# Two decoder layers on one core: other places for layer 0's value and gate splits, and norm sums as rows turned to columns

## The reference

```
for l in range(2):
    ada = silu(c) @ W_ada[l] + b_ada[l]     # shift, scale, gate for two sub-layers
    u = x*(1+sc1)+sh1;  x = LayerNorm(alpha*x + (1+g1)*Mixer(u))
    u = x*(1+sc2)+sh2;  x = LayerNorm(alpha*x + (1+g2)*SwiGLU(u))
```

## Time and profile before

| | us |
|---|---|
| runs (3) | 1695.4 median, 1695.18 to 1696.8 |
| profiled execution, its own time | 1694.97 |
| its span | 1693.2 |
| PE busy | 1629.9 (96%) |
| PEld busy | 1290.8 (76%) |
| DVE busy | 1001.0 (59%) |
| ACT busy | 623.4 (37%) |
| chain that ended last | PE 89%, DVE 5%, ACT 2%, DMA 1% |

### The profile page before, as it was taken

How to read it: one execution, slowest core, us unless ns; L and a number is a source line. 1 busy time by engine, 2 the same in 40 slices (tenths; PEclk the granted TensorE clock), 3 DMA queues, 4 the chain that set the end, 5 groups by cost and what they waited for, 6 DMA issues and landing times.

```text
span 1693.2 us, 21286 instructions
## 1 busy us (share of the span) xinstructions
PE 1629.9 (96%) x8391; PEld 1290.8 (76%) x8391; DVE 1001.0 (59%) x1548; ACT 623.4 (37%) x1117; POOL 51.6 (3%) x102
## 2 busy tenths in 40 slices
PE   6899999999999999999989999999999999999997
PEld 3678766677778888888878777766778788888886
DVE  3677677758676565555557657766557533333344
ACT  3332454444253332222253325445533533222221
POOL 1000000000000000000000000000000000000000
PEclk8999999999999999999999999999999999999999
DMA  9664221134327666665416331111223233334232
GB/s 306 186 183 138 75 63 52 50 100 132 107 60 211 186 188 187 186 184 149 148 51 191 87 88 38 39 38 31 82 87 100 62 100 99 100 96 122 88 94 73
DMA packets 278450, 193.07 MB, mean 114 GB/s; under 512 B 8344, under 2 KB 264912, under 8 KB 278352
## 3 DMA queue, kind: packets, MB, share of 16 engines
q1 hardware_dynamic: 264112, 147.95, 30.1%
q0 software_dynamic: 12320, 43.11, 8.6%
q10 hardware_dynamic: 1920, 0.66, 0.2%
HBM read 189.59 MB, written 2.10 MB: 113 GB/s over the span
## 4 chain that ended last, share of the span: by engine, by line
PE 89%; DVE 5%; ACT 2%; DMA 1%; issue 1%; SPq 0%; DVEq 0%; ACTq 0%
PE banks L1553 23%; PE banks L1555 22%; PE banks L1554 22%; PE banks L1671 3%; PE banks L1702 3%; PE banks L1730 2%; DMA ada_first<-in_w_ada_dram 1%; PE banks L1587 1%; PE banks L1588 1%; PE banks L1591 1%; PE banks L1606 1%; PE banks L1608 1%; PE banks L1607 1%; PE banks L1677 1%; PE banks L1681 1%
## 5 line engine op out<-in xcount | busy, mean ns | idle before, releaser
L1553 PE MATMUL banks<-u_hi,w_hi 128*128 128x512 f32 x1144 | 470.6, 411 | 14.9 <-DVE w_lo L941 11.6
L941 DVE TENSOR_TENSOR w_lo<-ring,w_hi 128x1024 fp32r<-128x1024 f32 (+2 forms) x246 | 294.4, 1199 | 309.6 <-ACT w_hi L687 308.3
L1555 PE MATMUL banks<-u_hi,w_lo 128*128 128x512 f32 x1144 | 449.2, 393 | 0.0
L1554 PE MATMUL banks<-u_lo,w_hi 128*128 128x512 f32 x1144 | 449.1, 393 | 0.0
L687 ACT ACTIVATE w_hi<-ring 128x1024 fp32r<-128x1024 f32 (+2 forms) x246 | 253.9, 1033 | 210.3 <-PE banks L1555 77.2
L1553 PEld LDWEIGHTS banks<-u_hi,w_hi 128*128 128x128 f32 x1144 | 216.5, 189 | 66.4 <-DVE w_lo L941 11.6
L1555 PEld LDWEIGHTS banks<-u_hi,w_lo 128*128 128x128 f32 x1144 | 216.3, 189 | 46.8
L1554 PEld LDWEIGHTS banks<-u_lo,w_hi 128*128 128x128 f32 x1144 | 217.3, 190 | 35.5
L833 ACT ACTIVATE probs<-banks,neg_max 128x128 f32<-128x128 f32 (+3 forms) x192 | 99.0, 524 | 159.6 <-DVE neg_max L1342 159.6
L1553 PE MATMUL banks<-h_hi,w_hi 128*128 128x512 f32 x352 | 138.5, 394 | 0.0
L1555 PE MATMUL banks<-h_hi,w_lo 128*128 128x512 f32 x352 | 137.0, 389 | 0.0
(11 more groups left out here) (240 smaller groups left out, 2159.3 us busy)
## 6 DMA issues: line engine op xcount, KB each, us to landing
ring<-in_w_ffn_in_dram SPq DMA_DIRECT2D x88, 512.0 KB, 3.9
ada_ring<-in_w_ada_dram POOLq DMA_DIRECT2D x80, 512.0 KB, 4.3
ring<-in_w_in_dram SPq DMA_DIRECT2D x72, 512.0 KB, 3.8
ring<-in_w_ffn_out_dram SPq DMA_DIRECT2D x32, 448.0 KB, 3.4
ada_first<-in_w_ada_dram SPq DMA_DIRECT2D x16, 512.0 KB, 8.3
ring<-in_w_out_dram SPq DMA_DIRECT2D x16, 512.0 KB, 3.6
ring<-in_w_ffn_out_dram SPq DMA_DIRECT2D x16, 512.0 KB, 4.1
w<-in_cmp_w_k_dram SPq DMA_DIRECT2D x8, 512.0 KB, 5.2
```

The costliest lines, as they stand in the source:

```text
L941: V.tensor_tensor(lo, src, hi.bitcast(fp32), ALU.subtract).then_inc(split_lo, 1)
L1553: M(bank, wh[:, block], sh[:, k, :], start=start, stop=False)
L1554: M(bank, wh[:, block], sl[:, k, :], start=False, stop=False)
L1555: return M(bank, wl[:, block], sh[:, k, :], start=False, stop=stop)
```

## The change

Four edits. (1) In layer 0 the splits of `vsg0`, `vsg1`, `vsg2` and `qn0` are placed by hand: VectorE does `vsg0` ahead of the set-up, `vsg1` between the two `build_flat`, `vsg2` behind them, `qn0` between the ropes of `ksl` and `kwn`; ScalarE does `vsg0` behind the copy of `kc`, `vsg1` ahead of `kwn`'s copy, `vsg2` and `qn0` behind it. The clearing of `v_cmp` moves up. (2) In the inner norms the sums are made by `rows`: 32 columns of `ones` stationary, 128 data columns moving, four groups of tokens into four groups of 32 partitions; VectorE copies the 128x128 result to `ln_rows`, TensorE transposes it, VectorE reads one column of each group. The order of the sums, the places of `keep_busy` (2, 2 and 7 instead of 8) and its bank change. (3) ScalarE's high half of the third job moves behind all squares; VectorE's low half is made in two halves, ahead of `u_lo` of block 0 and of block 1; `project_first` waits for each half where it reads it. (4) The sum of the last conditioning group moves from `kwn` to `qd3` of layer 1, its save from behind `qn1`'s rope to `vd1`.

```diff
-                "kwn": 9}
+ADA_SUM_WITH = {..., (0, "fo3"): 8, (1, "qd3"): 9}
...
+FIRST_LAYER_SPLIT = [(0, name) for name in ("kwn", "vsg0", "vsg1", "vsg2", "qn0")]
...
@@ scalar: layernorm
-                    if m == KD - 1 and not last:
-                        prepare(l + which, FIRST_SPLIT[which])
...
+                if not last:
+                    prepare(l + which, FIRST_SPLIT[which])
                 act.wait_ge(var_ready, n + 1)
@@ scalar: start of a layer
                 nc.scalar.activation(cmp_raw[:, 0, :], bank_of(l, "kc"), ACT.Copy)...
+                if l == 0:
+                    prepare(0, "vsg0")
...
                 for r, name in enumerate(RAW[:2]):
+                    if l == 0 and name == "kwn":
+                        prepare(0, "vsg1")
                     save_raw(l, name, r)
+                if l == 0:
+                    prepare(0, "vsg2")
+                    prepare(0, "qn0")
@@ vector: layernorm
-                if not last_norm:
-                    prepare(l + which, FIRST_SPLIT[which])
...
                 dve.wait_ge(mean_done, n + 1)
+                V.tensor_copy(ln_rows[:, 0, :], mean_rows).then_inc(mean_rows_saved, 1)
+                dve.wait_ge(var_done, n + 1)
+                V.tensor_copy(ln_rows[:, 1, :], square_rows).then_inc(square_rows_saved, 1)
+                dve.wait_ge(mean_col_turned, n + 1)
                 V.tensor_copy(mean_s, mean_col).then_inc(mean_saved, 1)
                 dve.wait_ge(mean_saved, n + 1)
                 link(V.tensor_tensor(square_s, mean_s, mean_s, ALU.mult))
-                dve.wait_ge(var_done, n + 1)
-                V.tensor_tensor(var_s, var_col, square_s, ALU.subtract).then_inc(var_ready, 1)
+                dve.wait_ge(square_col_turned, n + 1)
+                V.tensor_tensor(var_s, square_col, square_s, ALU.subtract).then_inc(var_ready, 1)
...
+                    if m in (1, 2):
+                        prepare_half(l + which, FIRST_SPLIT[which], m - 1)
                     if m:
                         sub_layer_low(n + 1, m - 1)
+            def prepare_half(l, name, half):
+                n, part = split_job(l, name), slice(half * SLOT // 2, (half + 1) * SLOT // 2)
+                ...
+                dve.wait_ge(split_hi, n + 1)
+                V.tensor_tensor(lo[:, part], src[:, part], hi[:, part].bitcast(fp32), ALU.subtract)\
+                    .then_inc((third_half, split_lo)[half], 1)
@@ vector: start of layer 0
             prepare(0, "kwn")
+            V.memset(v_cmp[:, :, :], 0.0)
+            prepare(0, "vsg0")
             V.memset(d_mix[:, 0:1], 0.0).then_inc(part1, 1)
...
                 build_flat(1)
+                if l == 0:
+                    prepare(0, "vsg1")
                 dve.wait_ge(kc2_ready, l + 1)
                 build_flat(0)
+                if l == 0:
+                    prepare(0, "vsg2")
...
                 for r, name in enumerate(("ksl", "kwn")):
                     prepare_behind(l, name)
+                    if l == 0 and name == "kwn":
+                        prepare(0, "qn0")
...
-                    elif i == 1:
-                        save_ada(9)
...
-                    if l == 0 and name == VD[1]:
-                        save_ada(0)
+                    if name == VD[1]:
+                        save_ada(9 * l)
@@ tensor: project_first
+                    for name, bank in zip(names, out):
+                        if name in THIRD and k == 0:
+                            pe.wait_ge(third_half, 2 * l + THIRD.index(name))
+                        elif k == (KD // 2 if name in THIRD else 0):
+                            take_split(l, name)
@@ tensor: mean_and_variance
+                def rows(out, src, start, stop):
+                    for i in range(TT):
+                        ins = M(out[32 * i:32 * i + 32, :], ones[:, 0:32], src[:, i * P:(i + 1) * P],
+                                start=start, stop=stop)
+                    return ins
...
                 pe.wait_ge(y_summed, n + 1)
-                columns(mean_col, t2, True, False)
+                rows(mean_rows, t2, True, False)
+                wait_saved(pe, l, ("wo", "fo")[which] + str(KD - 2))
+                keep_busy(2)
+                wait_saved(pe, l, ("wo", "fo")[which] + str(KD - 1))
+                rows(mean_rows, res[:, KD - 1, :], False, True).then_inc(mean_done, 1)
                 pe.wait_ge(sq_summed, n + 1)
-                columns(var_col, squares[:, 0, :], True, False)
-                wait_saved(pe, l, ("wo", "fo")[which] + str(KD - 1))
-                columns(mean_col, res[:, KD - 1, :], False, True).then_inc(mean_done, 1)
+                rows(square_rows, squares[:, 0, :], True, False)
                 pe.wait_ge(squared, (n + 1) * KD)
-                columns(var_col, squares[:, KD - 1, :], False, True).then_inc(var_done, 1)
+                rows(square_rows, squares[:, KD - 1, :], False, True).then_inc(var_done, 1)
+                pe.wait_ge(mean_rows_saved, n + 1)
+                nc.tensor.transpose(mean_turned, ln_rows[:, 0, :], ident).then_inc(mean_col_turned, 1)
+                pe.wait_ge(square_rows_saved, n + 1)
+                nc.tensor.transpose(square_turned, ln_rows[:, 1, :], ident).then_inc(square_col_turned, 1)
                 pe.wait_ge(mean_saved, n + 1)
                 spread(mean_ps, 0).then_inc(mean_spread, 1)
+                keep_busy(2)
                 pe.wait_ge(rstd_saved, n + 1)
                 spread(rstd_ps, 3).then_inc(rstd_spread, 1)
-                keep_busy(8)
+                keep_busy(7)
```

More of the change, by code:

```diff
@@ L136, in prepared_at @@
             nl, ni = divmod(l * len(SPLIT) + i + NQ - 1, len(SPLIT))
-            if nl < DEPTH and SPLIT[ni] not in FIRST_SPLIT and (nl, SPLIT[ni]) != (0, "kwn"):
+            if nl < DEPTH and SPLIT[ni] not in FIRST_SPLIT and (nl, SPLIT[ni]) not in FIRST_LAYER_SPLIT:
                 out.append((nl, SPLIT[ni]))
@@ L182 @@
 ADA_FFN = 3
-ADA_SUM_WITH = {"qd3": 0, "gm14": 1, "wo2": 2, "fb6": 3, "fb10": 4, "fb14": 5, "fb18": 6, "fb21": 7, "fo3": 8,
-                "kwn": 9}
-ADA_SUM_LAYER = {g: int(name == "kwn") for name, g in ADA_SUM_WITH.items()}
+ADA_SUM_WITH = {(0, "qd3"): 0, (0, "gm14"): 1, (0, "wo2"): 2, (0, "fb6"): 3, (0, "fb10"): 4, (0, "fb14"): 5,
+                (0, "fb18"): 6, (0, "fb21"): 7, (0, "fo3"): 8, (1, "qd3"): 9}
 FIRST = ("kc", "vc", "ksl")
@@ L257, in build @@
         w1_all = at("w1", 20, 16)
+        ln_rows = at("ln_rows", 16, 1)[:, 0, 0:2 * P].rearrange("p (k n) -> p k n", n=P)
         hid_rep_all = at("hid_rep", 8, 1)
@@ L358, in build @@
         rows_ps, cols_ps = banks[:, 6, :], banks[:, 7, :]
-        shift_ps, mean_col, var_col = banks[:, 2, :], banks[:, 3, 0:TT], banks[:, 4, 0:TT]
+        shift_ps = banks[:, 2, :]
+        mean_rows, square_rows = banks[:, 3, 0:P], banks[:, 4, 0:P]
+        mean_turned, square_turned = banks[:, 3, P:2 * P], banks[:, 4, P:2 * P]
+        mean_col, square_col = (b.rearrange("p (i n) -> p i n", i=TT)[:, :, 0] for b in (mean_turned, square_turned))
         third_ps, rstd_ps, mean_ps = banks[:, 5, :], banks[:, 6, :], banks[:, 7, :]
@@ L393, in build @@
         split_lo = sem("split_lo")
+        third_half = sem("third_half")
         part_read = sem("part_read")
@@ L436, in build @@
         sq_summed = sem("sq_summed")
+        mean_rows_saved = sem("mean_rows_saved")
+        square_rows_saved = sem("square_rows_saved")
+        mean_col_turned = sem("mean_col_turned")
+        square_col_turned = sem("square_col_turned")
         mean_saved = sem("mean_saved")
@@ L620, in load_slices @@
             def load_slices(first, last):
-                for n in range(first * KD, last * KD):
+                for n in range(first, last):
                     (l, j), k = ADA_GROUPS[n // KD], n % KD
@@ L1165, in _ @@
                                 1.0 - LAMBDA_INIT[l], None, ALU.mult)
-            V.memset(v_cmp[:, :, :], 0.0)
             dve.wait_ge(const_in, 32)
@@ L1519, in sum_ada @@
             def sum_ada(l, name, m):
-                g = ADA_SUM_WITH.get(name)
-                if g is None or ADA_SUM_LAYER[g] != l:
+                g = ADA_SUM_WITH.get((l, name))
+                if g is None:
                     return
@@ L1578, in project_first @@
             def project_first(l, names, src, high, ready, count):
-                w = [take_split(l, name) for name in names]
                 out = [take_bank(l, name) for name in names]
@@ L1585, in project_first @@
                     pe.wait_ge(high, count + k + 1)
-                    for bank, (wh, wl) in zip(out, w):
+                    for name, bank in zip(names, out):
[3 more added lines that the diff above has]
+                            take_split(l, name)
+                        wh, wl = split_slot(l, name)
                         M(bank, wh[:, block], sh[:, k, :], start=k == 0, stop=False)
@@ L1589, in project_first @@
                     pe.wait_ge(ready, count + k + 1)
```

(7 more changed lines are left out.)

4 lines of the change are left out of this document (3 added, 1 removed).

## The result

The changed kernel takes 1685.8 us (median of 4 runs, 1684.9 to 1686.8), the kernel before 1696.1 beside it (4 runs, 1695.2 to 1697.8): ratio 0.9935, 95% interval 0.9923 to 0.9947. The forecast was 1685.2. The profiled execution took 1685.16 with a span of 1683.3, against 1694.97 and 1693.2: 9.9 us of span to explain, 10.2 had been forecast.

A forecast was written before the change was run, and what follows sets the result against it. TensorE, busy 96% of the span, was taken as the bound, so only its gaps and clock matter. Gains 6.8 + 3.1 + 0.3 = 10.2 off 1694.97 give 1684.8, median 1685.2 us; range 1682.0 to 1689.3.

The forecast's parts named there:

- Part 1: Layer 0's value splits: earlier low halves on VectorE close TensorE's wait at the value products; gain 6.8 us.
- The rival of a late landing: Layer 0: `vsg2` or `qn0` lands 6 us or more behind issue, TensorE waits at `qn0`; 1688.7 us, chance 0.09.
- Part 2: Inner norms' sums as `rows`, 0.42 us each: first real product's L1102 1.4 us earlier at full clock, 0.6 at low.
- the 1.2 us that I had set beside the sum: Inner norms: two tiling switches on the path per norm, 0.19 each, 1.2 us less gain over three norms; left out.
- Parts 2 and 3: Inner norms: sums as `rows` plus third block's low half in two loop pieces; together 3.1 us over three norms.
- the middle: Gain per inner norm taken as 1.05 us, between 1.5 at full clock and 0.6 to 0.7 at low.
- Part 4: Last conditioning group's eight transposes leave layer 1's `kwn`, at low clock, for a full-clock place: gain 0.3 us.
- if the gap behind the norm then starts warm: Addition to the clock-up rival: clock high at the gap behind the norm, somewhat faster still, 1682 instead of 1683.0 us.
- 5.54 + 24 x 0.096: Layer 0's values: upper bound of the gain if every wait went, given as 7.9 us.
- the clock stays up in all norms: Rival: full clock in all norms and no wait left at `qn0`; 7.9 + 4.2 + 0.3, 1683.0 us, chance 0.10.
- The halves eat the norms' gain: Rival: slower copies and turns, or low clock in all three norms, leave the norm edits about zero; 1688.3 us, chance 0.18.
- The slower one: Rival: four groups of `rows` run in line at low clock, 5.0 us a norm lost; 1703.3 us, chance 0.03.

The follow-up runs named there:

- splits alone: The kernel before with only layer 0's new split places and the moved clearing of `v_cmp`: 1688.2 us, ratio 0.9951.
- columns kept: The changed kernel with all four norm sums by `columns`, no copies, turning or idle pairs, eight idle products behind the spreads: 1691.2 us, ratio 0.9966.
- whole third block ahead: The changed kernel with the third job's high half back ahead of ScalarE's square and both low-half pieces ahead of the statistics: 1685.4 us, ratio 0.9933.
- last group at its old place: The changed kernel with the last conditioning group's transposes back at `kwn` of layer 1: 1682.3 us, ratio 0.9919.
- in the gap: The changed kernel with the last conditioning group's eight transposes in layer 1's idle gap behind `project_first`: 1684.0 us, ratio 0.9924.
- `kwn` first: The changed kernel with ScalarE making `kwn`'s high half ahead of the copies of `kc` in layer 1: 1682.1 us, ratio 0.9909.

## Why the prediction was right, and where it was not

**Part 1 was right in size and place.** Forecast 6.8, measured 6.65 to 6.7 in two kernels. The steps, with this execution 1.6 us later at the start: values forecast from 61 to 73.5, seen from 62.62 to 75.08; 0.13 apart; waits at `qn0` and `qn1` forecast at 0.5 and 0.7, seen 0.46 and 0.44. The low halves were ready at 58.27, 66.43, 69.07, 75.65 and about 81.85 (`vsg0` to `qn1`), which is 1.67, 1.63, 1.37, 1.75 and 1.75 behind the forecast: all of it the late start, to 0.3. VectorE's queue, summed job by job from its own rows, gives this stretch. The rival of a late landing fell: ScalarE waited for two landings (4.01 and 2.46 us) but had `vsg2`'s high half done at 68.1 and `qn0`'s at 71.6, with VectorE there at 68.3 and 74.4, for `vsg2` with only 0.2 us to spare.

**Part 2, the size of a `rows` was right:** 0.42 forecast, 0.42 and 0.43 seen. The Trainium skill, page TensorEngine Tiling (Array Packing), section Key Properties, has a change of tiling mode drain TensorE. Here the first `rows` starts 0.32 us behind the product before it (475.29 to 475.61), where two products are 0.23 apart, so at this switch the trace shows 0.1 us at the most, and the 1.2 us that I had set beside the sum for that rule did not come.

**Parts 2 and 3 were right in the steps, and took the wrong share of the clock.** The reciprocal was forecast at 3.3 and the first L1102 at 4.1 to 4.9 behind the last add (3.27 and 4.26 seen), the end of `project_first` at +23.1 (504.0), seen +23.26. But the gain I took was the middle of 1.5 (full clock) and 0.6 to 0.7 (low), 1.05 a norm; measured were 1.32, 1.28 and 0.95 (3.55 against 3.1). The step that failed is the middle: the clock stays up in every norm with rows and the seven idle products (three norms in each of ten profiled executions) and fell in every norm with columns (three in each of three: before, splits alone, columns kept).

And most of the gain is this clock, which I had held for a modifier of it. I compared an end at the high level with one that had run at the low and put the difference down to the shorter chain. The whole third block ahead shows it: its reciprocal is at +4.06, as in the splits alone (+4.07), so nothing is earlier when the spreading starts; yet its first norm ends at +23.43 and theirs at +24.74. The splits alone, then the whole third block ahead:
```profile
480.55 3.65 PE L1795 MATMUL banks<-merged_hi 128*128 128x512 f32 x8
481.72 0.82 ACT L696 ACTIVATE u_hi<-res,add_u,mul_u 128x512 fp32r<-128x512 f32 x1 [1.86 <-DVE res L1110]
...
484.04 0.40 PE L1602 MATMUL banks<-u_hi,w_hi 128*128 128x512 f32 x1
```
```profile
480.73 1.87 PE L1828 MATMUL banks<-merged_hi 128*128 128x512 f32 x7
481.80 0.81 ACT L704 ACTIVATE u_hi<-res,add_u,mul_u 128x512 fp32r<-128x512 f32 x1 [1.75 <-DVE res L1123]
482.87 0.47 PE L1626 MATMUL banks<-u_hi,w_hi 128*128 128x512 f32 x1 [0.28 <-ACT u_hi L704]
```
At the low level the eight idle products took 3.65 us and kept TensorE from the first real product until 484.04, 1.50 us after its `u_hi` was ready (482.54). At the high level the seven were through in 1.87, at 482.60, just as `u_hi` was ready (482.61); an eighth, at 0.23, would by this estimate still have ended ahead of the first product. That product comes at +8.21 and at +6.85, which is the 1.31 but for 0.05. So what the low clock cost in the old norm it cost through the idle products, which stood in the way; in the kernel before likewise (`u_hi` ready at +7.05, first product at +8.10). Whether the old sums with fewer idle products, or with none, would have given a part of this gain was not run and stays open.

The chain that is 0.8 us shorter adds 0.17. In the changed kernel `project_first` is held by VectorE's `u_lo` of block 1 (TensorE idles 0.19 for it at +10.05), which starts at +9.31, and at +9.33 with the third block ahead, where TensorE comes to it at +10.35 without a wait: work that is taken from ahead of the statistics and put into the loop delays `u_lo` by what it saved.

What keeps the clock up, rows or idle products, is half answered. With the four `rows` and no idle products the clock fell in one of three norms; with columns and eight idle products behind the spreads it fell in three of three. So the rows (with their copies and turning) matter most, the seven idle products perhaps something, on the one norm that fell, the two pairs nothing. Why one norm fell and two did not, at the same instructions, is open.

**Part 4 had the wrong sign**, and this is the step of the prediction that failed in its mechanism: "the clock was still low ..., for a place at the full clock: 0.3 us". I compared two prices of the transposes and did not ask what covered them. At `qd3` nothing does. The changed kernel there:
```profile
973.59 0.39 PE L1589 MATMUL banks<-u_hi,w_lo 128*128 128x512 f32 x1
973.82 0.27 PE L1565 MATMUL banks<-cst,ada_acc 128*128 128x128 f32 x1
973.85 0.47 PE L1587 MATMUL banks<-u_hi,w_hi 128*128 128x512 f32 x1
974.16 0.39 PE L1588 MATMUL banks<-u_lo,w_hi 128*128 128x512 f32 x1
...
974.62 0.27 PE L1565 MATMUL banks<-cst,ada_acc 128*128 128x128 f32 x1
```
From one transpose to the next are 0.80 us, where three products alone take 0.68: 0.125 each, 1.0 for the eight. At `kwn` they stood in front of value products that wait for VectorE anyway, so they cost nothing. Two experiments bear it out (147.01 at the old place, 147.08 in the gap, 148.12 at `qd3`).

**The sum came out so close by luck.** Forecast 10.2: 6.8, 3.1, 0.3. Measured: 6.7, 3.55, -1.1, then 1.7 behind the third norm, where the clock stays up behind the gap of 2.57 (my rival "if the gap behind the norm then starts warm" had 1.0 for it), 0.7 in small differences that I traced to no edit (0.2 ahead of the first norm, 0.5 in layer 1), less 1.65 at the start. The 1.65 is no work of the change: the changed kernel itself starts at 55.62 in one execution and at 54.05 in the other. The 1.7 cannot be called its work either: behind the third norm the clock stayed up with the columns kept, and fell with the last group at its old place and with `kwn` first, whose norms are the changed kernel's. Without the 1.65 the span would have been 11.5 shorter. Two small sums of the prediction are off and move nothing: 5.54 + 24 x 0.096 is 7.84 and not 7.9, and three norms at 1.5 are 4.5 where the rival has 4.2.

Of the rivals, "the clock stays up in all norms" held for the norms; its other half did not (the wait at `qn0` was 0.46), and it had 4.2 us for the three norms, which gave 3.55, and no loss in Part 4. "The halves eat the norms' gain" was true of the shortened chain (0.17 of the 0.8 left) and false of the time. The slower one asked for 2.3 us a norm; none was near.

## What to carry to other kernels

Before a few instructions are moved off a queue that waits, ask what covers them at the old place and at the new one: eight transposes of 0.125 us were free ahead of a wait, cost 1.1 us in a full stretch and were free again in a gap. Where a gap of the bounding engine is closed or shortened, count the clock behind it as well, and ask whether another engine then lets it be used: in layer 1 the full clock was worth nothing while VectorE's low half of `vsg2` set the pace, and with the splits placed earlier the stretch behind the gap gave more (3.7 us) than the gap itself (3.1). Idle products that are to hold the clock stand in the way when it falls all the same: eight took 3.65 us in front of work that was ready. And when a chain is shortened by moving work behind it, the gain is what is left at the next place where the two engines meet, here the second block's low half.

## What the runs showed of the hardware

- The sum over 128 partitions of 128x512, as eight products: 1.03 us with one moving column each at the high clock, 1.85 at the low; 0.42 to 0.43 as rows with 32 stationary columns in four groups.
- The stretch at the low level, behind a gap or in a norm, was 3.4 or 6.8 us long in all profiles, but for the start and the end of the span. Behind a gap of 2.57 us it came in some executions and not in others, with the same code. Behind the one of 5.22 it came in every one (ten executions, 3.4 or 6.8 us); in the same place it came behind 4.34 (one execution, transposes in front of it) and did not behind 2.08 (one) or 1.21 (two).
- In the norms the clock fell in nine of nine with sums as columns (three profiled kernels), in none of thirty with rows and seven idle products (ten executions), in one of three with rows and no idle products.
- The changed kernel's runs spread over 1681.9 to 1686.7 us. Two places of 1.6 us each, at the start and behind the first norm, separate its two profiled executions; an effect of 1 us has to be read from markers within the trace and not from the medians.
